# Placing GpSimd's selections between low halves, and scoring two attention heads side by side, in a two-layer float32 kernel

## The reference, cut to what matters

```python
logit = einsum('hqd,hkd->hqk', q, k) * dh ** -0.5 - slopes * dist   # causal
p = softmax(logit)
out = einsum('hqk,hkd->hqd', p, v) * silu(a_z)
```

```python
sc = einsum("thpk,hpnk->thpn", (t @ w_q).reshape(...), sub_keys)
s_top, i_top = top_k(sc, 16)                       # for each half
best, pos = top_k(all sums of the two halves, 16)
idx = take_along_axis(i_top[0] * 128 + i_top[1], pos)
g = softmax(best)
act = gelu(einsum("phkd,pd->phk", u_tab[idx], t))  # then g * act with v_tab
```

## Time and profile before

| | value |
|---|---|
| median of three runs | 2410.72 us |
| profiled execution, its own time | 2405.64 us |
| its span | 2403.9 us |
| TensorE busy | 2158.7 us, 90% |
| VectorE busy | 1690.5 us, 70% |
| ScalarE busy | 819.6 us, 34% |
| GpSimd busy | 771.1 us, 32% |
| granted TensorE clock, mean | 0.952 |

### The profile page before, as it was taken

How to read it: one execution, slowest core, us unless ns; L and a number is a source line. 1 busy time by engine, 2 the same in 40 slices (tenths; PEclk the granted TensorE clock), 3 DMA queues, 4 the chain that set the end, 5 groups by cost and what they waited for, 6 DMA issues and landing times. The chain is left out here.

```text
span 2403.9 us, 36262 instructions
## 1 busy us (share of the span) xinstructions
PE 2158.7 (90%) x11207; PEld 1887.0 (78%) x11207; DVE 1690.5 (70%) x3352; ACT 819.6 (34%) x1408; POOL 771.1 (32%) x677
## 2 busy tenths in 40 slices
PE   5998988475999997796979999999998999999997
PEld 4776677364777776686879999999997888888885
DVE  3675545536877763499478888788876888888886
ACT  4443322212222230423424444444432333333333
POOL 1000033000000000147546877887753222222220
PEclk9998999787999998898989999999998999999999
DMA  4431100013424222602256878878688999999995
GB/s 112 83 70 36 18 1 0 22 58 87 112 63 126 63 55 70 199 20 78 95 178 228 295 249 273 295 254 267 227 299 304 333 335 339 337 337 339 336 339 205
DMA packets 229948, 428.88 MB, mean 178 GB/s; under 512 B 18516, under 2 KB 155892, under 8 KB 229620
## 3 DMA queue, kind: packets, MB, share of 16 engines
q1 hardware_dynamic: 170976, 254.85, 34.1%
q0 software_dynamic: 41472, 151.01, 18.3%
q10 hardware_dynamic: 17428, 22.14, 2.6%
HBM read 381.80 MB, written 46.14 MB: 178 GB/s over the span
## 5 line engine op out<-in xcount | busy, mean ns | idle before, releaser
L1847 PE MATMUL bank<-xt_hi,u_hi 128*128 128x384 f32 x896 | 309.3, 345 | 0.0
L2127 PE MATMUL bank<-xt_hi 128*128 128x512 f32 x768 | 302.3, 394 | 7.6 <-DVE xt_lo L2056 7.6
L1847 PE MATMUL bank<-xt_hi,u_lo 128*128 128x384 f32 x896 | 300.6, 336 | 0.0
L1847 PE MATMUL bank<-xt_lo,u_hi 128*128 128x384 f32 x896 | 300.1, 335 | 0.0
L2127 PE MATMUL bank<-xt_hi,xt_lo 128*128 128x512 f32 x768 | 299.8, 390 | 0.0
L2127 PE MATMUL bank<-xt_lo,xt_hi 128*128 128x512 f32 x768 | 299.8, 390 | 0.0
L1709 POOL DMA_INDIRECT row_slot<-in_peer_v_dram,row_index x128 | 139.2, 1088 | 392.7 <-DVE row_x L2060 373.4
L2103 ACT ACTIVATE xt_hi<-xh 128x1024 fp32r<-128x1024 f32 x128 | 135.8, 1061 | 338.4 <-PE bank L2127 332.9
L1378 POOL TENSOR_TENSOR k_wlo<-k_raw,k_whi 128x2048 fp32r<-128x2048 f32 x4 | 18.4, 4604 | 615.8 <-ACT k_whi L1498 615.8
L2053 DVE TENSOR_TENSOR xt_lo<-xh,xt_hi 128x1024 fp32r<-128x1024 f32 x128 | 156.9, 1226 | 83.8 <-ACT xt_hi L2103 82.4
L1788 POOL TENSOR_TENSOR u_two<-u_match,u_weight_hi 128x512 fp32r<-128x512 f32 x96 | 179.7, 1872 | 96.8 <-DVE u_match L1874 96.3
(11 more groups left out here) (430 smaller groups left out, 4908.1 us busy)
## 6 DMA issues: line engine op xcount, KB each, us to landing
xh<-in_peer_v_dram SPq DMA_DIRECT2D x128, 512.0 KB, 5.4
xh<-in_peer_u_dram SPq DMA_DIRECT2D x113, 512.0 KB
x_raw<-in_w_in_dram SPq DMA_DIRECT2D x56, 512.0 KB, 7.0
v_ga<-acts SPq DMA_DIRECT2D x128, 192.0 KB, 5.4
acts<-xh ACTq DMA_DIRECT2D x112, 192.0 KB
weights<-u_spread POOLq DMA_DIRECT2D x32, 512.0 KB
v_gg<-weights SPq DMA_DIRECT2D x128, 128.0 KB
p_raw<-in_w_in_dram SPq DMA_DIRECT2D x12, 1024.0 KB
```

The lines of the kernel that those rows point to most:

```text
L1847: mm = pe.matmul(k.ps[4 + b][:, 0:DENSE], w[b][:, c, :], x[:, c, 0:DENSE], start=(c == 0 and w is uhi and x is hi), stop=(c == DC - 1 and ...
L2127: mm = pe.matmul(k.ps[q][:, :], h[b][:, t * P:(t + 1) * P], v[b][:, f], start=False, stop=False, skip_group_check=True)
```

## The change

In the attention the order of steps changes so that the two heads of a pair with the same query tile follow each other, and TensorE issues two scores at every second step, one on partitions 0 to 63 and one on 64 to 127. In the choice of experts GpSimd's selections are put at other places between the early low halves: before, both of step 1 came ahead of low half 0, those of step 2 behind low halves 4 and 14; after, low halves 0 and 1 lie between the two of step 1, and those of step 2 come behind low halves 6 and 8. Nothing is added or removed.

```diff
-        steps = [(p, b, qt) for p in range(2) for b in range(2) for qt in range(TT)]
+        steps = [(p, b, qt) for p in range(2) for qt in range(TT) for b in range(2)]
...
                     for n in range(n_steps):
-                        if n + 2 < n_steps:
+                        if n % 2 == 0 and n + 2 < n_steps:
                             score(i, n + 2)
+                            score(i, n + 3)
                         project(i, n, 0)
...
                 low(pool, 7)
-                select(1, 0)
-                select(1, 1)
 
                 def low_early(e):
                     pool.wait_ge(u_copied, after(4 * (e + 1)))
                     pool.tensor_tensor(u_lo[e % 4], u_turn[e % 2], u_hi[e % 4].bitcast(F32), ALU.subtract).then_inc(u_low, 1)
-                for e in range(5):
+                select(1, 0)
+                for e in range(2):
+                    low_early(e)
+                select(1, 1)
+                for e in range(2, 7):
                     low_early(e)
                 select(2, 0)
-                for e in range(5, EARLY - 1):
+                for e in range(7, 9):
                     low_early(e)
                 select(2, 1)
-                low_early(EARLY - 1)
+                for e in range(9, EARLY):
+                    low_early(e)
```

## The result

The changed kernel takes 2373.09 us (median of four runs, 2370.27 to 2374.62), the kernel before 2408.24 (2404.75 to 2411.18, with a new run beside it). The ratio is 0.9853, 95% interval 0.9834 to 0.9873: 35 us less, and faster clear of noise. The direction and the expert choice were right; the attention gained three times what I gave it.

What follows compares the result with a forecast made beforehand. GpSimd's last selection was taken to set the expert choice's end, TensorE to bound the attention. From 2405.64 us, 21 and 4.5 off gave 2380.1; with the median 5.08 above the profiled execution, 2385, range 2376 to 2396.

Steps and rivals of the forecast that it cites:

- Part 1: Expert choice: GpSimd's selections moved among the low halves let products start earlier and end VectorE's wait; gain 21 us.
- One cover: End of expert choice: VectorE's work, stretched by GpSimd's low halves, done at 1187, some 4 us ahead of the exponential.
- Rival B: End of expert choice: low halves stretch VectorE's last 14 us to 1193 or later; gain 14 to 18, time 2390; chance 0.12.
- rival E: Expert choice: moving the selections changes little because the end hangs elsewhere; time 2406; chance 0.03.
- Part 2: Attention: adjacent scores of two heads save fixed costs, overlap passes and fill waits, less new waits; gain 4.5 us.
- The fixed term: Attention: a pair of adjacent scores pays 0.31 us once instead of twice; 16 pairs, 5 us.
- The upper bound of 12.7: Attention: the most gained, in us, with fixed costs, overlap and filled waits in full and nothing given back.
- The waits: Attention, TensorE waiting for the exponential: eight waits of 0.44 filled, 3.5 us gained; new ones cost 4 to 8, taken as 6.
- The rule that I cited: Attention: matmuls on different row groups run concurrently but start and end strictly in program order; overlap 4.2 us, sum 2383.
- A, the full overlap: Attention: overlap and filled waits come in full, little given back; gain 9 to 12 us, time 2378; chance 0.13.
- C: Attention gives nothing or loses up to 3 us, waits for ScalarE summing to over 12 us; time 2391; chance 0.11.
- D: Attention: new TensorE gaps pull its granted clock to the lower level; slower, 2415 us; chance 0.03.

Runs made afterwards that it cites:

- e4: The changed kernel with the old order of steps, two scores at every second step on the same 64 rows: attention 115.9 us; 2374.63 us in one run.
- e3: The changed kernel with the new order of attention steps but one score at each step, none adjacent: attention 127.5 us, one run.
- e2: The changed kernel with the attention of before again, only GpSimd's selections moved: 2387.46 us, ratio 0.9922 to the kernel before; attention 123.9 us.
- e5: The changed kernel with each score of the loop's pairs made twice, first head, first, second, second: attention 116.2 us; eight passes take 1.92 us.

## Why the prediction was right or wrong

**Part 1 was right**, 21 forecast, 21.4 measured. With the stage's start 12.4 us earlier in the trace of after, the forecast's dates read: product 0 at 1099.9 (measured 1087.5 + 12.4 = 1099.9), product 2 at 1114.1 (1114.5), product 7 at 1142 (1142.8), product 9 at 1156.3 (1157.4), the exponential's end at 1190.9 (1191.3). One cover was mis-sized on the safe side: VectorE was done at 1180.1 where I had 1187, and had 11.2 us of room where I gave it 4. Its last 13.6 us of work were stretched by 2.1 only, all of it in the masks (6.69 us for 4.5), and before they had taken 15.5 as well. In the products after them it was GpSimd that took longer, 3.96 us for a low half of 2.4. Rival B is out, and rival E as well.

**Part 2 failed in one term**, that the passes of two heads overlap "between 0 and 4.2, and I take half". I let only the second pass of one head overlap the first of the other. Both do: a pair costs one score, and saves two passes instead of one, 2 x 4.2 = 8.4 us. Of the 9.0 us that the attention gained beyond my 4.5, 6.4 are this term. The fixed term holds in its price (e4), but there are 14 new pairs and not 16, 4.3 us instead of 5: the first two scores of each half, `score(i, 0)` and `score(i, 1)`, stood side by side before as well, on the same rows. The upper bound of 12.7 was built on the same 4.2 and so was too low as well.

The waits came out as forecast. I had added 3.5 us for waits removed and taken 6 for new ones, net 2.5 given back; measured over the stage they grew by 2.4. That the net fits so well is in part luck: by e4, 2.2 were removed and 4.6 new ones came, both less than I had. Each term is seen by itself: with the old order of steps the second score did fill the waits of 0.44 (e4), and the new order puts new ones in, of 0.78 and 0.54 in a turn of eight steps (e3 and after). In such a turn at the high clock the work that went is (0.42 + 0.63 + 0.84 + 1.05) + 4 x 0.10 = 3.3 us, the waits grew from 0.88 to 1.32, and 25.8 less 22.9 is the 2.9 that these give.

Over the stage, 8.4 and 4.3 are 12.7 of the 15.9 us by which TensorE's busy time fell. The other 3.2 I had not in the sum. They go with the clock: by its share in the stage, 0.903 and 0.922, TensorE ran 23.8 us of the attention at 1.2 GHz before and 17.1 after. By the projection matmul's two prices, 0.42 and 0.24, 6.7 us less at that level are worth up to 2.9. Whether the change causes this isn't shown: e2 has the attention of before, 31 us at that level, and took 1.1 longer.

The rest of the miss is the starting point. Against 2385 the result is 11.9 us lower: 9.0 are the attention, 0.4 the expert choice, and 2.5 come from the median of before, 2410.72 on record and 2408.24 with the new run.

The rule that I cited from the Trainium skill ("TensorE: Matmul & The Clock Gate", "The mechanism") is half borne out: matmuls on different row groups run side by side. Its strict program order isn't: by it the overlap would be 4.2 where it was 8.4, and e5 take 2.7 us where it took 1.92.

Rivals: A, the full overlap, came nearest with 2378, but for the same reason fell 5 us short of the gain. C and D are out: the waits for the exponential sum to 7.2 us and not to 12, and the clock rose a little.

## What to carry to other kernels

Where two matmuls use half of the rows each, put those on different halves next to each other: here the second, of the same width, was free, float32 passes included, and the fixed cost of a score was paid once. When an engine waits for one item of another engine's queue, lay that queue out again with the durations of the trace; that forecast the dates of the products here to about a microsecond, and missed the end of VectorE's work by 7, where a guess about a shared resource went in. Bound an unseen overlap by the case that everything overlaps, not by the order that the program is written in.

## What the runs showed of the hardware

A float32 matmul of 64 rows shows as two passes of 0.43 us for 512 columns at the high clock, and a pair on different rows starts both heads' passes within 0.01 us of each other. Doubled scores, written head by head, took the time of four passes: the second head's first score ran beside the first head's first one, 0.014 us behind it, and not after the first head's second one as written (e5). The prediction had allowed for neither.
